# Two transformer blocks on one core: cleared tiles on TensorE and an early table load at the opening, half a low part on VectorE, an old half on ScalarE at the end

## The reference

```python
# first block: norm, projection to 4104 columns, two mixers, output projection
h = rms_norm(x, norm_pre_w)                    # x: 512 x 1024
proj = h @ w_in                                # a_q..a_z, d_q, d_k, d_v, d_z (512 each), d_b, d_a (4 each)
qkv = silu(causal_depthwise_conv(concat(d_q, d_k, d_v), conv_w))
...                                            # block attention, gated delta rule
x = x + rms_norm(mixed @ w_out, norm_post_w)
# second block: HGRN2 and sparse attention, merged, then
h = h + square(relu(rmsnorm(h, norm2_g) @ w_ff1)) @ w_ff2
return rmsnorm(h, final_g)
```

## Time and profile before

| | us |
|---|---|
| median of three runs | 1227.01 (1225.25 to 1227.77) |
| profiled execution, device time | 1227.18 |
| its span, first to last instruction | 1225.4 |
| TensorE matmuls busy | 1186.3 (97%) |
| VectorE busy | 638.0 (52%) |
| ScalarE busy | 315.8 (26%) |
| GpSimd busy | 678.1 (55%) |

### The profile page before, as it was taken

One profiled execution on the slowest core, in us unless ns is written; L12 is line 12 of the kernel. 1 busy time (PEld: TensorE's weight loads), 2 busy tenths in 40 slices (PEclk: granted clock), 3 DMA queues, 4 the chain that ended last, 5 costly groups with the idle time before them and its releaser, 6 DMA issues.

```text
span 1225.4 us, 18867 instructions
## 1 busy us (share of the span) xinstructions
PE 1186.3 (97%) x6848; PEld 976.9 (80%) x6848; DVE 638.0 (52%) x1222; ACT 315.8 (26%) x668; POOL 678.1 (55%) x610
## 2 busy tenths in 40 slices
PE   7999999998998999999899999999999999999997
PEld 6777778777877877877788888878888888888885
DVE  3887554687823575553876657571453300335022
ACT  3125122124631323211235444410221100113001
POOL 4885343444536586765633333366576666666662
PEclk9999999999999999999999999999999999999998
DMA  7231111114013222224521111122333333233321
GB/s 247 87 86 52 53 52 52 53 53 121 2 36 99 81 86 86 69 78 142 203 69 52 37 52 52 53 69 87 90 98 103 89 101 103 86 103 106 100 86 69
DMA packets 29684, 102.41 MB, mean 84 GB/s; under 512 B 3632, under 2 KB 6064, under 8 KB 28848
## 3 DMA queue, kind: packets, MB, share of 16 engines
q1 hardware_dynamic: 27232, 93.47, 24.7%
q10 hardware_dynamic: 2384, 7.99, 2.0%
HBM read 95.16 MB, written 2.10 MB: 79 GB/s over the span
## 4 chain that ended last, share of the span: by engine, by line
PE 84%; DVE 7%; POOL 4%; issue 2%; ACT 2%; DMA 1%; SPq 0%; DVEq 0%; POOLq 0%; ACTq 0%
PE acc L281 23%; PE acc L282 22%; PE acc L283 22%; POOL w_lo L1552 3%; PE aux L494 3%; PE aux L1627 3%; PE aux L484 2%; PE aux L348 1%; PE aux L1609 1%; PE aux L876 1%; PE aux L877 1%; DMA residual<-x 1%; PE aux L789 1%; DVE conv_sum L1962 1%; PE acc L494 0%
## 5 line engine op out<-in xcount | busy, mean ns | idle before, releaser
L1544 POOL CAST w_hi<-w_raw 128x1024 fp32r<-128x1024 f32 x164 | 178.0, 1085 | 497.1 <-issue 358.6
L1552 POOL TENSOR_TENSOR w_lo<-w_raw,w_hi 128x256 fp32r<-128x256 f32 x352 | 292.3, 860 | 7.1
L281 PE MATMUL acc<-ht_hi,w_hi 128*128 128x512 f32 x672 | 271.9, 405 | 6.1 <-DVE ht_lo L392 2.3
L283 PE MATMUL acc<-ht_hi,w_lo 128*128 128x512 f32 x672 | 263.9, 393 | 0.0
L282 PE MATMUL acc<-ht_lo,w_hi 128*128 128x512 f32 x672 | 263.7, 392 | 0.0
L1547 POOL TENSOR_TENSOR w_lo<-w_raw,w_hi 128x1024 fp32r<-128x1024 f32 x76 | 188.0, 2473 | 6.1
L281 PEld LDWEIGHTS acc<-ht_hi,w_hi 128*128 128x128 f32 x672 | 126.9, 189 | 36.7 <-POOL w_lo L1552 6.0
L283 PEld LDWEIGHTS acc<-ht_hi,w_lo 128*128 128x128 f32 x672 | 127.1, 189 | 27.5
L282 PEld LDWEIGHTS acc<-ht_lo,w_hi 128*128 128x128 f32 x672 | 127.4, 190 | 23.8 <-issue 0.7
L281 PE MATMUL acc<-w_hi,ht_hi 128*128 128x512 f32 x256 | 105.9, 414 | 0.3
L281 PE MATMUL acc<-w_hi,ff_hi 128*128 128x512 f32 x256 | 100.4, 392 | 2.3 <-POOL w_lo L1547 2.3
(11 more groups left out here) (425 smaller groups left out, 1928.3 us busy)
## 6 DMA issues: line engine op xcount, KB each, us to landing
w_raw<-units SPq DMA_DIRECT2D x164, 512.0 KB, 3.5
cmp_w<-w_kv ACTq DMA_DIRECT2D x4, 1024.0 KB, 6.8
residual<-x SPq DMA_DIRECT2D x4, 512.0 KB, 7.0
k_turned<-k_split SPq DMA_DIRECT2D x8, 256.0 KB, 3.7
result<-normalized SPq DMA_DIRECT2D x4, 512.0 KB, 2.6
consts_sb<-consts SPq DMA_DIRECT2D x1, 1120.5 KB, 7.0
k_turned<-k_split ACTq DMA_DIRECT2D x2, 512.0 KB, 6.1
norm_post_sb<-norm_post ACTq DMA_DIRECT2D x1, 512.0 KB, 6.0
```

The costliest lines, as they stand in the source:

```text
L281: nc.tensor.matmul(bank, ah, bh, start=start, stop=False)
L283: return nc.tensor.matmul(bank, al, bh, start=False, stop=stop)
L1544: nc.gpsimd.tensor_copy(w_hi[:, slot], raw[:, j]).then_inc(hi_split, 1)
L1552: done = nc.gpsimd.tensor_tensor(w_lo[:, slot, kk, cols], raw[:, j, kk, cols], w_hi[:, slot, kk, cols].bitcast(F32), ALU.subtract)
```

## The change

- TensorE: waits for a new semaphore `zeros_ready` and does seven 128x512 matmuls of cleared tiles into `aux3` before it waits for the identity.
- VectorE: clears `w_ba_lo` and `w_ba_hi` at its very start, no longer behind the row copy. Between low chunks 0 and 1 it computes the first half of unit 0's low part (from SBUF); GpSimd computes only the second half. Before it splits the small weights it waits for `row_summed`.
- ScalarE: one activation on one column stands before its first wait for a turned chunk, and with it the table load.
- SyncE: waits for low chunk 1 before it refills the ring (the slot of unit 0 is now read by VectorE too). The small weights count on `consts_in`, whose wait goes from 16 to 32.
- The end: the old half of tile 3 is scaled by ScalarE, and SyncE waits for both engines at each tile.

```diff
@@ opening_slab
-            pe.wait_ge(consts_in, 16)
+            pe.wait_ge(consts_in, 32)
@@ ScalarE, end
                 if t:
                     first_half_scaled(t - 1)
+            first_half_scaled(NT - 1)
@@ VectorE, end
             scaled(NT - 1)
-            V.tensor_scalar(xn[:, NT - 1, 0:NC], xn[:, NT - 1, 0:NC], last_y[NT - 1], None,
-                            ALU.mult).then_inc(on["final_n"], 1)
@@ SyncE, end
-                if t < NT - 1:
-                    sp.wait_ge(on["final_s"], t + 1)
-                    sp.wait_ge(on["final_n"], t + 1)
-                else:
-                    sp.wait_ge(on["final_n"], NT + 1)
+                sp.wait_ge(on["final_s"], t + 1)
+                sp.wait_ge(on["final_n"], t + 1)
@@ SyncE, opening
-            sp.dma_start(wba[:].rearrange("p k n -> p (k n)"), w_ba).then_inc(small_in, 16)
+            sp.dma_start(wba[:].rearrange("p k n -> p (k n)"), w_ba).then_inc(consts_in, 16)
...
+            sp.wait_ge(flip_lo, FLIP1 + 2)
             units_in(1, keys_first)
@@ GpSimd, split
-                if pieces == 1:
+                if isinstance(unit, int) and unit == 0:
+                    done = nc.gpsimd.tensor_tensor(w_lo[:, slot, 1], raw[:, j, 1], w_hi[:, slot, 1].bitcast(F32),
+                                                   ALU.subtract)
+                elif pieces == 1:
@@ TensorE
+            pe.wait_ge(zeros_ready, 1)
+            for _ in range(7):
+                nc.tensor.matmul(aux[3][:], wba_lo[:, 0], wba_lo[:, 0:4].rearrange("p k n -> p (k n)"), start=True,
+                                 stop=True)
             pe.wait_ge(ident_in, 16)
@@ ScalarE
             act.wait_ge(params_in, 16)
+            nc.scalar.activation(small(364, 1), param("norm_pre"), ACT.Square)
@@ VectorE
+            step(V.memset(wba_lo[:].bitcast(F32), 0.0))
+            V.memset(wba_hi[:].bitcast(F32), 0.0).then_inc(zeros_ready, 1)
...
-            for k in range(4):
+            flip_lo_chunk(eng, ht_hi, ht_lo, 0, FLIP1, lambda k: param("norm_pre", k))
+            eng.wait_ge(raw_in[0], 16)
+            eng.wait_ge(hi_split, 1)
+            V.tensor_tensor(w_lo[:, 0, 0], raw[:, 0, 0], w_hi[:, 0, 0].bitcast(F32), ALU.subtract)
+            for k in range(1, 4):
                 flip_lo_chunk(eng, ht_hi, ht_lo, k, FLIP1, lambda k: param("norm_pre", k))
...
-            eng.wait_ge(consts_in, 16)
-            eng.wait_ge(small_in, 16)
-            step(V.memset(wba_hi[:].bitcast(F32), 0.0))
-            step(V.memset(wba_lo[:].bitcast(F32), 0.0))
+            eng.wait_ge(consts_in, 32)
+            eng.wait_ge(row_summed, 1)
```

More of the change, by code:

```diff
@@ L236, in two_blocks @@
         wait_passed = sem("wait_passed")
-        small_in = sem("small_in")
+        zeros_ready = sem("zeros_ready")
         raw_in = [sem(f"raw_in{j}") for j in range(RING)]
```

## The result

The changed kernel takes **1228.85 us** (median of 22 runs, 1226.87 to 1232.99), the kernel before beside it 1227.58 (22 runs): a ratio of 1.0014, 95% interval [1.0008, 1.0021]. By the ratio that is slower by 1.7 us (the two medians lie 1.3 apart). It is inside the 0.2% that the prediction called the same, and inside its range, but it is not no change: the forecast of 1227.0 misses it by more than the measurement's own uncertainty. The profiled execution took 1229.05, with a span of 1227.2.

What follows compares the result with a forecast made beforehand. VectorE's chain from x's last quarter, blocked by GpSimd, was taken to hold unit 2, with TensorE only 0.1 us ahead. All terms summed to 0, so 1227.0 us was forecast, range 1225.3 to 1229.0.

Steps and rivals of the forecast that it cites:

- Zeros: Opening, TensorE: seven matmuls from 3.4 delay the turning to 6.4 to 6.5, but the slab's six matmuls take 1.35, not 2.70.
- The first rival: TensorE's first slab starts at the low clock all the same: +0.5 to +1.0 us, chance 0.12.
- Table and half: Opening: early table load saves 1.28 us, first chunk at 7.6, VectorE's half takes 0.7, first real matmul at 10.7.
- The collision: Opening: VectorE's half meets GpSimd's rounding of unit 1; if second, it ends 0.55 us behind the rounding.
- the second rival: Opening: VectorE's half stands behind GpSimd's rounding of unit 1, making TensorE late for unit 2: +0.6 to +2.0 us, chance 0.10.
- Unit 2: TensorE's start of unit 2 still waits for VectorE's low chunk 5: 24.1 to 24.3, priced -0.1 to +0.2, taken 0.
- a blocked time that only changes its victims: Ahead of unit 2: VectorE still loses 2.9 to 3.1 us to GpSimd's rounding and subtraction, against 2.9 before.
- Memsets moved, end: Memsets behind the row copy free 2.1 us under cover: 0. Last store issued 0.2 earlier, landing longer: -0.2 to 0, taken 0.
- chance of the clock elsewhere: Beyond the opening: a shift by some tenths may lose or add a 1.6 us clock drop; chance 0.06, half each side.

Runs made afterwards that it cites:

- e2: Kernel before plus the early memsets, the seven matmuls on zeros and the wait for row_summed: 1228.64 us, ratio 1.0012.
- e1: Changed kernel without its seven matmuls on zeros, the memsets staying at VectorE's start: 1228.95 us, ratio 1.0017 to the kernel before.
- e4: Changed kernel with GpSimd's subtraction of unit 2 in four pieces instead of one: 1228.72 us, ratio 1.0009 to the kernel before.
- e6: Changed kernel with one more memset of an unused column behind its two early memsets: 1226.90 us, ratio 0.9997 to the kernel before.
- e10: Kernel before with three memsets of unused columns at VectorE's start: 1226.95 us, ratio 0.9996.
- e11: Changed kernel with unit 2's subtraction in four pieces and one more unused memset: 1227.48 us, ratio 1.0003 to the kernel before.
- e14: Kernel before with two unused memsets at VectorE's start and a third just ahead of the last delta tile's preparation: 1227.65 us, ratio 0.9998.
- e12: Kernel before with 130 memsets of one column at VectorE's start: 1229.24 us, ratio 1.0009.

## Why the prediction was wrong

- **Zeros.** From 3.83 (predicted 3.4), 0.48 us each (0.45); turning from 6.98 (6.4 to 6.5). The 16 turning matmuls took 2.26 us, and the slab ran at 0.23 us a matmul from its start: the upper level (2.4 GHz), in spite of 1.53 us of idle time ahead. The first rival, low clock at the slab, didn't come; e2 shows it behind 1.97 us. Right.
- **Table and half.** First chunk at 7.90 (7.6), half 0.68 (0.7), first real matmul at 10.77 (10.7). Right. The collision came the other way round: VectorE's half came first and GpSimd's rounding of unit 1 waited and took 1.47, which nobody needed. In e1 and e4 VectorE came second and took 1.2 to 1.3. In e1 unit 2 was still released by VectorE; in e4, where it stood behind the rounding of unit 1 as in the second rival, TensorE reached unit 2 at 24.24 and set its time, so the rival's path exists but cost nothing that can be told, not +0.6.
- **Unit 2.** At 24.48 behind a wait of 0.64 (predicted 24.1 to 24.4, 0.4 to 1.0): it came 0.25 later where I took 0. That isn't the term: the landing of x was 0.2 later, and from VectorE's first step to its low chunk 4 it is 6.3 us in both (16.48 to 22.78, 16.70 to 23.02). The mechanism, a blocked time that only changes its victims, is what the rows show: now the steps of 1.03 and 2.25 us stand behind GpSimd. e4 confirms it by taking 1.4 us of it away. Right.
- **Memsets moved, end.** Taken at 0 each. The end measured 0.9998; the memsets have no cost at equal clock, with an interval that leaves room for one.
- **The step that failed** is one that the sum didn't have. Each edit was costed by its duration and by who waits for it, and behind 38 us the forecast had nothing but the end and a "chance of the clock elsewhere", at 0.06. That VectorE's half brings two entries to an instruction stream, and that these move the multiplication of gdn_DEC to a number at which it starts late, was missing: 0.56 us in the trace, 0.8 by the runs. "In an idle engine, so free" held for the engine's time and not for its place in the code.
- **The clock** had a rival of its own, with a chance that was too small: some 0.7 us go with it, and its cause isn't known.

A rule of the Trainium skill stands against what was measured. Runtime: NRT & Kernel Launch (Instruction fetch mechanics) says that crossing from one block of instructions to the next is "mostly hidden", with blocks of 16 KiB, which are 256 instructions. For VectorE these traces show 8 KB and a period of 128, and a crossing, if that is what stands at these places, that is hidden in a run of long instructions but costs 0.35 to 0.38 us behind a wait that is already over.

## What to carry to other kernels

An instruction that costs nothing where it stands still moves the number of every later instruction of its engine, and here that cost or saved half a microsecond at a place 250 us away. When a small edit moves the time by about 0.1% and its own stage doesn't explain it, compare the starts of one regular operation over the whole span, find where the distance steps, and put in one, two or three idle instructions ahead: if the step comes and goes with their number, the edit's work was innocent of it. Differences of 0.3 us in one stage of a single profile are no lead: kernels with the same opening differed by that much. Tuning of this size is worth nothing unless the count is redone at the end.

## What the runs showed of the hardware that I hadn't expected

- Of VectorE's instructions (waits counted), every one numbered 82 + 128 n that stood behind a wait of 0.02 us and found the engine idle started 0.35 to 0.38 us late: two or three of them in each of twelve kernels, 27 in all, without an exception, against none of 3094 at other numbers. In the other four (e6, e10, e11 and e14) no entry of these numbers stands behind such a wait, and none is late. In e12 a run of memsets, 0.03 us apart, stood still for 0.39 us ahead of number 63, without a wait.
- An idle time of 1.91 us of TensorE near 105 us was followed by the low clock in eight profiles of sixteen and not in the other eight, with the same instructions around it. At the first slab it fell behind 1.97 us in e2, and in e4 it held its upper level (a granted clock of 1.00 from 11.3 to 20 us) behind 2.20.
- VectorE can hold GpSimd too: in the changed kernel a rounding that takes 1.04 us elsewhere took 1.47 beside a VectorE product with two SBUF inputs.
- TensorE at the upper level after matmuls of cleared tiles kept it over 16 turning matmuls and 1.53 us of idle time.
